# First stages merged into the block of the first head product, and the last layer norm merged into the last feed-forward

## The chip, the cores and the metric

The kernel runs on 1 core of one Trainium2 chip. A core has five engines with a queue of instructions each: TensorE (PE: matrix products and transposes; its weight loads are listed as PEld), VectorE (DVE), ScalarE (ACT), GpSimd (POOL) and SyncE (SP), which here only issues DMA transfers. Engines wait for each other on counting semaphores. The metric is the device time of one execution in microseconds (us); lower is better. The time shown is the median of 3 runs.

## The reference

Two blocks of two layers each run over 512 latent tokens and 256 context tokens of width 1024, in float32. Cut to what the change touches:

```python
# first block, layer 0: the modulation comes out of c, then x is normed and modulated
mod_l = split((silu(c) @ w_mod[i] + b_mod[i])[:, None, :], 6)      # shift, scale, gate, ...
h_l = modulate(rms_norm(x, norm1_g[i]), mod_l[0], mod_l[1])        # h * (1 + scale) + shift
q, k, v = h_l @ w_qkv ...                                          # the first head product
lam = exp(sum(lq1 * lk1)) - exp(sum(lq2 * lk2)) + lam_init

# second block, end of its last layer: feed-forward, residual, layer norm, result
y = layer_norm(ALPHA * x + gate * (square(relu(h @ w1)) @ w2), ln_ff_g, ln_ff_b)

def layer_norm(x, g, b):
    mu = mean(x); var = mean(square(x - mu))
    return (x - mu) * rsqrt(var + LN_EPS) * g + b
```

`rms_norm` is per row of x: it needs x alone, not the modulation. The modulation of layer 0 that the first product needs (shift and scale) is the first 2048 columns of `w_mod`.

## The kernel before

Tokens lie on the 128 partitions: x is six tiles of 128 x 1024 (four latent, two context). Every weight matrix streams through as halves of 128 x 4 x 512 (1024 KB): SP loads a half into `raw[h]`, ACT writes its rounded part `w_hi[h]` (`split_hi`), DVE the rest `w_lo[h]` (`split_lo`), and PE makes each product from three (hi x hi, lo x hi, hi x lo). `raw[h]` is loaded again once the semaphore `lo_done` says that `split_lo` has read it.

The program is a row of blocks. Between two blocks all engines meet at a barrier. Inside `together(K)` several stages share one block, and each engine walks from one stage into the next without a barrier. The order of work is the order of the code on each engine; no planner is involved.

The start has four blocks before:

- The memsets (L887 to L896).
- `start_stage`. SP issues small vectors, the four blocks `mod_first0` to `mod_first3` of `w_mod` (128 x 8 x 512, 2048 KB each), then x (2048 KB) and the context (1024 KB), then both halves of slab 0 and of slab 1 of the first weight stream, and last a bias table that goes to DRAM (`rel_table_rest`), for whose landing it waits. PE multiplies c with each block (`mod_rows`, L852), ACT copies the row out (`first_rows`), PE turns it into columns (`mod_turns`, L860), DVE sums and adds the bias (`mod_sums` L866, `mod_add` L873). ACT and DVE split both halves of slab 0.
- `lambda_stage`: four small DVE operations and one on ACT.
- The `together` block with `scale_stage`, `operand_stage` and `heads_gemm_stage`. `Norm.roots` on ACT takes square, sum and root of each tile of x (L312, L314), `Norm.rest` on DVE the reciprocal (L275) and the scaled tile `xhat` (L282). PE transposes `xhat` (L239), ACT applies scale and shift (`feat`, L804), DVE splits that into `hT_hi` (L761) and `hT_lo` (L763), one of eight groups of 128 features (k = 0 to 7) at a time. PE turns k = 0 to 3 ahead and the others between the products of the first slab's first half (L362 to L364).

`K.held` names a slab whose second half is not split yet when an operand stage begins. `operand_stage` then splits it behind k = 5 on ACT and on DVE. In other places of the program this is in use; at the start it isn't before.

The end has two blocks. In the last chunk of `mlp_stage`, PE makes two halves of the down product for four tiles; DVE multiplies each result with the gate (`scaled_buf`, L535) and POOL adds it to x (L543). Then comes a block of its own, `layer_norm_stage`: statistics of the four tiles on DVE (L1864, L1866), one root on ACT (L1885), and two passes over each tile on DVE (L1869, L1875), behind each of which SP stores the tile.

`Norm.beside` is a way to take a norm inside a product stage, in use elsewhere in the program: behind the gate multiply of tile j (last chunk, second half) DVE takes the statistics of tile j - 1 and writes the normed tile j - 2.

Of the kernel before, what the change touches and what calls it, by code (L numbers as in the profile page):

```python
# [242 lines left out]
class Norm:  # L243


    def __init__(self, K, kind, tiles, out):
        self.kind, self.tiles, self.out = kind, tiles, out
        self.n = len(tiles)
        self.added = None
        self.seen = self.scaled = 0  # L250
# [18 lines left out]
    def normalise(self, K, dve):  # L269
# [29 lines left out]
    def roots(self, K, act):  # L299

        act.preload_act_table(ACT.Sqrt)
        link = Chain(act, K.act_chain)
        for j, t in enumerate(self.tiles):
# [8 lines left out]
            link(act.activation(K.relu_mlp[:, :, :].rearrange("p a b -> p (a b)"), K.x[:, t, :], ACT.Square,  # L312
# [62 lines left out]
def ahead_loop(eng, stage, body, hold=False):  # L375
# [10 lines left out]
    if stage.last:  # L386
# [159 lines left out]
def mlp_stage(K, stream, nxt, tiles, mod=None, hold=False, norm=None):  # L546
# [183 lines left out]
    K.held = st.g0 + 2 * chunks if hold else None  # L730
# [146 lines left out]
def start_stage(K, x, ctx, first, w_mod, groups, rpb, lambdas):  # L877
# [3 lines left out]
    blocks = 4  # L881
    rows = w_mod.rearrange("(k p) n -> p k n", p=P)
    ld0 = [s.n for s in K.mod_loaded]
    us0, tr0, cn0, sm0, ro0, mt0, dc0 = (s.n for s in (K.mod_used, K.turned, K.c_done, K.small_loaded, K.row_out, K.mod_turned,
                                                       K.dve_chain))
    n_vectors = sum(len(g) for g in groups)
# [11 lines left out]
    with nc.Block() as block:  # L898
        @block.sync
        def _(sp):  # L900
            sp.dma_start(K.ident[:, :], K.c_ident).then_inc(K.ident_loaded.h, 16)
# [21 lines left out]
        def _(act):  # L923

            act.wait_ge(K.c_done.h, cn0 + 1)
            act.activation(K.cexp[:, :], K.vecs[:, 0:4 * KD], ACT.Exp, scale=-1.0).then_inc(K.c_done.h, 1)
            for b in range(blocks):
                act.wait_ge(K.mod_used.h, us0 + b + 1)
                act.activation(K.first_rows[:, b, :], K.bank[b][:, :], ACT.Copy).then_inc(K.row_out.h, 1)
            for h in range(2):  # L930
                act.wait_ge(K.raw_loaded[h].h, 16)
                act.activation(K.w_hi[h][:, :, :], K.raw[h][:, :, :], ACT.Copy).then_inc(K.hi_done.h, 1)
            act.wait_ge(K.inputs_loaded.h, 32)

        @block.vector
        def _(dve):
# [17 lines left out]
            ins.then_inc(K.c_done.h, 1)  # L954
            for b in range(blocks):
# [3 lines left out]
            for h in range(2):  # L959
                split_lo(K, dve, 0, h)  # L960
# [3 lines left out]
        def _(pe):  # L964
# [7 lines left out]
            for b in range(blocks):  # L972
                pe.wait_ge(K.mod_loaded[b].h, ld0[b] + 16)
                mod_rows(K, pe, K.bank[b], 0, K.mod_first[b][:, :, :]).then_inc(K.mod_used.h, 1)
# [9 lines left out]
    K.c_done.n += 3  # L984
    K.small_loaded.n += 16 * n_vectors
# [517 lines left out]
def attention_stage(K, units, q_of, k_of, values, out, diff=False, bias=False, sink=False, mod=None):  # L1503
# [35 lines left out]
    with nc.Block() as block:  # L1539
# [6 lines left out]
        elif mod:  # L1546
            @block.sync
            def _(sp):
                for v, p in rows_at.items():
                    if p >= 1:  # L1550
                        sp.wait_ge(K.pt_done[0].h, at(K.pt_done[0], order[v - len(units) // PAIRS, "mod"]))
                    sp.dma_start(K.mod_slab[:, :, :], mod.w[:, :, (mod.first + 4 * p) * P:(mod.first + 4 * p + 4) * P])\
                      .then_inc(K.mod_loaded[0].h, 16)
                    skew_bias(K, sp, (2 * p, 2 * p + 1))
# [285 lines left out]
def layer_norm_stage(K, gain, bias, tiles, store=None, gate=None, gate_scale=1.0):  # L1840


    nc = K.nc
    n = len(tiles)
    classes = 2 if n > LAT_TILES else 1
    mm0 = K.mm_done.n
    sm0, st0, sd0, rs0, ga0 = K.small_loaded.n, K.sums_done.n, K.std_done.n, K.rstd_done.n, K.gained.n
    with nc.Block() as block:
        @block.sync
        def _(sp):  # L1850
            sp.dma_start(K.ln_gain[:, :], gain.partition_broadcast(P)).then_inc(K.small_loaded.h, 16)
            sp.dma_start(K.ln_bias[:, :], bias.partition_broadcast(P)).then_inc(K.small_loaded.h, 16)
            if store is not None:
                for i, t in enumerate(tiles):
                    sp.wait_ge(K.gained.h, ga0 + i + 1)
                    sp.dma_start(store[t * P:(t + 1) * P, :], K.x[:, t, :]).then_inc(K.stored.h, 16)
                sp.wait_ge(K.stored.h, K.stored.n + 16 * n)

        @block.vector
        def _(dve):  # L1860
            link = Chain(dve, K.dve_chain)
            for i, t in enumerate(tiles):
                for h in range(2):
                    ins = dve.bn_stats(K.ln_stats[:, t, h, :], K.x[:, t, h * 512:(h + 1) * 512])  # L1864
                    link(ins)
                dve.bn_aggr(K.ln_mv[:, t, :], K.ln_stats[:, t, :, :]).then_inc(K.sums_done.h, 1)  # L1866
            dve.wait_ge(K.small_loaded.h, sm0 + 32)
            for i, t in enumerate(tiles):
                link(dve.scalar_tensor_tensor(K.x[:, t, :], K.x[:, t, :], K.ln_mv[:, t, 0:1], K.ln_gain[:, :],  # L1869
                                              ALU.subtract, ALU.mult))  # L1870
                if i == 0:
                    dve.wait_ge(K.std_done.h, sd0 + 1)
                    dve.reciprocal(K.rstd[:, 0:n], K.lnms[:, 0:n]).then_inc(K.rstd_done.h, 1)  # L1873
                    dve.wait_ge(K.rstd_done.h, rs0 + 1)
                dve.scalar_tensor_tensor(K.x[:, t, :], K.x[:, t, :], K.rstd[:, t:t + 1], K.ln_bias[:, :], ALU.mult, ALU.add)\  # L1875
                   .then_inc(K.gained.h, 1)
            K.dve_chain.n += link.k

        @block.scalar
        def _(act):  # L1880
            act.preload_act_table(ACT.Sqrt)
            if gate is not None:
                gate_evacuations(K, act, mm0, classes, gate_scale)
            act.wait_ge(K.sums_done.h, st0 + n)
            act.activation(K.lnms[:, 0:n], K.ln_mv[:, 0:n, 1], ACT.Sqrt, bias=K.eps_ln[:, 0:1]).then_inc(K.std_done.h, 1)  # L1885
        if gate is not None:
            @block.tensor
            def _(pe):
                for cls in range(classes):
                    gate_rows(K, pe, gate, cls)  # L1890
    if gate is not None:
        K.mm_done.n += classes
        K.gate_done.n += 2 * classes
    K.small_loaded.n += 32
    for s in (K.sums_done, K.gained):
        s.n += n
    K.std_done.n += 1
    K.rstd_done.n += 1
    if store is not None:
# [1346 lines left out]
```

## Time and profile before

| | us |
|---|---|
| median of 3 runs | 4089.12 |
| lowest and highest | 4088.18, 4091.37 |
| the profiled execution | 4090.46 |
| its span | 4088.7 |
| PE busy | 3773.7 (92%) |
| DVE busy | 1986.6 (49%) |
| ACT busy | 1330.2 (33%) |
| POOL busy | 807.5 (20%) |

The span is what the trace covers, from the first instruction to the last event; the profiled execution's own time is 1.76 us longer. PE is busy in nearly all of the span, so the places where it isn't are the ones to look at: in the page's picture of 40 slices (102 us each) the first slice of PE is 3 tenths. The last one is 7.

### The profile page before, as it was taken

The numbers are of one execution on the slowest core, as the hardware profiler recorded it, in microseconds if no ns is written. First come the engines' busy times: TensorE is split into PE (matmuls) and PEld (weight loads), VectorE is DVE, ScalarE is ACT, GpSimd is POOL, SyncE is SP. The second block draws the span as 40 slices with busy tenths as digits, with TensorE's granted clock in tenths as the row PEclk, the third lists the DMA queues.
The fourth block names the chain that finished last, engine by engine and source line by source line (L and its number), as shares of the span: only waits on it lengthen the run. The fifth ranks groups of instructions, "written<-read, shape, count | busy, mean of one in ns | idle before, by whom it ended". The sixth has DMA issues, their size and how long they took to land. (4 is left out here: it accounts for less than half of the span.)

```text
span 4088.7 us, 54795 instructions
## 1 busy us (share of the span) xinstructions
PE 3773.7 (92%) x20683; PEld 3018.8 (74%) x20683; DVE 1986.6 (49%) x2911; ACT 1330.2 (33%) x2276; POOL 807.5 (20%) x604
## 2 busy tenths in 40 slices
PE   3998889999999899999999999999999988898997
PEld 2875578888877667777776678888878865577776
DVE  2746644333354375443436654333356727746444
ACT  2335533212143354322325522122224324432222
POOL 0510011221222111122220011212110018701222
PEclk8999989999999899999999999999999998999999
DMA  4125303322312220444320013323211140032222
GB/s 159 55 72 150 98 31 115 122 92 97 118 52 72 83 53 32 175 144 154 103 75 3 2 42 128 123 92 123 92 62 52 55 144 14 19 103 83 92 92 72
DMA packets 191734, 352.34 MB, mean 86 GB/s; under 512 B 41980, under 2 KB 43597, under 8 KB 191565
## 3 DMA queue, kind: packets, MB, share of 16 engines
q1 hardware_dynamic: 189277, 346.07, 25.7%
q10 hardware_dynamic: 2304, 4.20, 0.3%
q8 instruction: 100, 1.64, 0.2%
q14 instruction: 53, 0.43, 0.0%
HBM read 341.71 MB, written 16.92 MB: 88 GB/s over the span
## 5 line engine op out<-in xcount | busy, mean ns | idle before, releaser
L543 POOL TENSOR_TENSOR x<-x,scaled_buf 128x512 f32<-128x512 f32 (+1 forms) x360 | 466.8, 1301 | 2335.4 <-DVE scaled_buf L535 2334.8
L129 DVE TENSOR_TENSOR w_lo<-raw,w_hi 128x2048 fp32r<-128x2048 f32 x198 | 457.8, 2312 | 827.9 <-ACT w_hi L123 809.7
L123 ACT ACTIVATE w_hi<-raw 128x2048 fp32r<-128x2048 f32 x196 | 375.3, 1915 | 1223.6 <-PE psum L364 1221.2
L362 PE MATMUL psum<-hT_hi,w_hi 128*128 128x256 f32 (+1 forms) x1920 | 677.6, 353 | 3.3 <-DVE hT_lo L763 2.5
L363 PE MATMUL psum<-hT_lo,w_hi 128*128 128x256 f32 (+1 forms) x1920 | 673.9, 351 | 0.0
L364 PE MATMUL psum<-hT_hi,w_lo 128*128 128x256 f32 (+1 forms) x1920 | 673.8, 351 | 0.0
L362 PE MATMUL psum<-w_hi,uT_hi 128*128 128x512 f32 x1280 | 512.4, 400 | 17.1 <-DVE uT_lo L614 17.1
L535 DVE TENSOR_TENSOR scaled_buf<-psum,gate 128x512 f32<-128x512 f32 x360 | 246.9, 690 | 538.5 <-PE psum L364 533.7
L364 PE MATMUL psum<-w_hi,uT_lo 128*128 128x512 f32 x1280 | 506.3, 396 | 0.0
L363 PE MATMUL psum<-w_lo,uT_hi 128*128 128x512 f32 x1280 | 506.3, 396 | 0.0
L362 PE MATMUL psum<-w_hi,hT_hi 128*128 128x512 f32 x1072 | 420.0, 392 | 8.3 <-ACT qkv L1250 5.9
L364 PE MATMUL psum<-w_hi,hT_lo 128*128 128x512 f32 x1072 | 417.5, 390 | 0.0
L363 PE MATMUL psum<-w_lo,hT_hi 128*128 128x512 f32 x1072 | 417.4, 389 | 0.0
L362 PEld LDWEIGHTS psum<-hT_hi,w_hi 128*128 128x128 f32 x1920 | 364.2, 190 | 52.6 <-DVE hT_lo L763 2.9
L363 PEld LDWEIGHTS psum<-hT_lo,w_hi 128*128 128x128 f32 x1920 | 364.1, 190 | 48.4
L364 PEld LDWEIGHTS psum<-hT_hi,w_lo 128*128 128x128 f32 x1920 | 363.5, 189 | 48.7
L362 PEld LDWEIGHTS psum<-w_hi,uT_hi 128*128 128x128 f32 x1280 | 240.7, 188 | 88.8 <-DVE uT_lo L614 24.0
L364 PEld LDWEIGHTS psum<-w_hi,uT_lo 128*128 128x128 f32 x1280 | 240.7, 188 | 57.9
L363 PEld LDWEIGHTS psum<-w_lo,uT_hi 128*128 128x128 f32 x1280 | 240.8, 188 | 54.2
L362 PEld LDWEIGHTS psum<-w_hi,hT_hi 128*128 128x128 f32 x1072 | 201.5, 188 | 51.7 <-ACT qkv L1250 7.5
L364 PEld LDWEIGHTS psum<-w_hi,hT_lo 128*128 128x128 f32 x1072 | 201.3, 188 | 41.9
L363 PEld LDWEIGHTS psum<-w_lo,hT_hi 128*128 128x128 f32 x1072 | 201.4, 188 | 40.8
(279 smaller groups left out, 4775.7 us busy)
## 6 DMA issues: line engine op xcount, KB each, us to landing
mod_wide<-in_w_mod SPq DMA_DIRECT2D x24, 3072.0 KB, 10.6
raw<-in_w_mlp SPq DMA_DIRECT2D x64, 1024.0 KB, 5.3
raw<-in_ff_w SPq DMA_DIRECT2D x64, 1024.0 KB, 5.3
raw<-in_ssm_w_in SPq DMA_DIRECT2D x20, 1024.0 KB, 5.1
mod_slab<-in_w_mod SPq DMA_DIRECT2D x8, 2048.0 KB, 8.1
raw<-in_a_w_qkv SPq DMA_DIRECT2D x12, 1024.0 KB, 5.1
raw<-in_b_w_qkv SPq DMA_DIRECT2D x12, 1024.0 KB, 5.1
mod_first<-in_w_mod SPq DMA_DIRECT2D x4, 2048.0 KB, 17.9
```

Source lines behind the costliest of these rows:

```text
L123: act.activation(K.w_hi[h][:, :, :], K.raw[h][:, :, :], ACT.Copy).then_inc(K.hi_done.h, 1)
L129: dve.tensor_tensor(K.w_lo[h][:, :, :], K.raw[h][:, :, :], K.w_hi[h][:, :, :].bitcast(F32), ALU.subtract).then_inc(K.lo_done.h, 1)
L362: pe.matmul(out, hi_a, hi_w, start=first, stop=False, **check)
L363: pe.matmul(out, hi_a, lo_w, start=False, stop=False, **check)
L364: return pe.matmul(out, lo_a, hi_w, start=False, stop=last, **check)
L535: dve.tensor_tensor(K.scaled_buf[:, j % 2, :], bank[:, :], K.gate[:, cls, ds(n * SLAB_N, SLAB_N)], ALU.mult)\
L543: pool.tensor_tensor(x, x, K.scaled_buf[:, j % 2, :], ALU.add).then_inc(K.added.h, 1)
```

## The change

- The memsets stay in a block of their own (`clear_stage`). `start_stage` moves into the `together` block, the lambda operations move into it, and the barriers between fall away. PE waits at its end for DVE's chain of sums.
- SP's order: x and the context come ahead of the modulation blocks; there are three buffers for the four modulation blocks, so the fourth is loaded into the first buffer once PE has read it. The bias table goes out in the midst of them. Slab 0's second half is loaded once all roots are taken (their squares go to that buffer), slab 1 behind it.
- The roots of x come ahead of the `first_rows` copies on ACT; the scaled tiles come on DVE behind the third block's product and ahead of the sums. They are written to `xhat_far`, which doesn't overlap the three buffers.
- Slab 0's second half is split as a held half (`K.held = 0`).
- The last layer norm becomes a `Norm` of kind "layer" with gain and bias rows, taken beside the last chunk's gate multiplies and finished in `store_stage`, in the same block. The two rows are loaded earlier, behind the last operand.

```diff
 class Norm:
     def normalise(self, K, dve):
...
-        if self.kind == "layer":
+        if self.rows is not None:
+            gain, bias = self.rows
+            link = Chain(dve, K.dve_chain)
+            if j == 0:
+                dve.wait_ge(K.small_loaded.h, self.loaded)
+            link(dve.scalar_tensor_tensor(self.out[:, t, :], K.x[:, t, :], K.ln_mv[:, t, 0:1], gain[:, :], ALU.subtract, ALU.mult))
+            ins = dve.scalar_tensor_tensor(self.out[:, t, :], self.out[:, t, :], K.rstd[:, t:t + 1], bias[:, :], ALU.mult, ALU.add)
+            K.dve_chain.n += link.k
+        elif self.kind == "layer":
...
 def start_stage(...)
-            for b in range(blocks):
-                sp.dma_start(K.mod_first[b][:, :, :], rows[:, :, b * SLAB_N:(b + 1) * SLAB_N]).then_inc(K.mod_loaded[b].h, 16)
             sp.dma_start(K.x[:, 0:LAT_TILES, :], x.rearrange("(t p) n -> p t n", p=P)).then_inc(K.inputs_loaded.h, 16)
             sp.dma_start(K.x[:, LAT_TILES:TOK_TILES, :], ctx.rearrange("(t p) n -> p t n", p=P)).then_inc(K.inputs_loaded.h, 16)
-            for n in range(2):
-                for h in range(2):
-                    load_half(K, sp, n, h, first.half(n, h), first=n == 0)
+            mod_block(0)
             sp.wait_ge(K.dve_chain.h, dc0 + 1)
             sp.dma_start(K.rel_dram.rearrange("(h r c) -> h r c", r=REL_ROWS + 2, c=P), K.rel_table[:, :, :]).then_inc(K.rel_loaded.h, 16)
-            sp.wait_ge(K.rel_loaded.h, 32)
+            mod_block(1)
+            mod_block(2)
+            load_half(K, sp, 0, 0, first.half(0, 0), first=True)
+            sp.wait_ge(K.mod_used.h, us0 + 1)
+            mod_block(3)
+            sp.wait_ge(K.std_done.h, norm.sd0 + norm.n)
+            load_half(K, sp, 0, 1, first.half(0, 1), first=True)
+            for h in range(2):
+                load_half(K, sp, 1, h, first.half(1, h))
...
         def _(act):
+            act.wait_ge(K.dve_chain.h, dc0 + 5)
+            act.activation(K.lam_sum[:, :], K.lam_sum[:, :], ACT.Exp).then_inc(K.act_chain.h, 1)
+            act.wait_ge(K.inputs_loaded.h, 32)
+            norm.roots(K, act)
             for b in range(blocks):
                 act.wait_ge(K.mod_used.h, us0 + b + 1)
                 act.activation(K.first_rows[:, b, :], K.bank[b][:, :], ACT.Copy).then_inc(K.row_out.h, 1)
-            for h in range(2):
-                act.wait_ge(K.raw_loaded[h].h, 16)
-                act.activation(K.w_hi[h][:, :, :], K.raw[h][:, :, :], ACT.Copy).then_inc(K.hi_done.h, 1)
-            act.wait_ge(K.inputs_loaded.h, 32)
+                if b == 2:
+                    act.wait_ge(K.raw_loaded[0].h, 16)
+                    act.activation(K.w_hi[0][:, :, :], K.raw[0][:, :, :], ACT.Copy).then_inc(K.hi_done.h, 1)
...
         def _(dve):
+            dve.wait_ge(K.inputs_loaded.h, 32)
+            dve.wait_ge(K.mod_used.h, us0 + 3)
+            norm.rest(K, dve)
+            split_lo(K, dve, 0, 0)
             for b in range(blocks):
                 dve.wait_ge(K.mod_turned.h, mt0 + b + 1)
                 link(mod_sums(K, dve, K.bank[b], 4))
                 link(mod_add(K, dve, 0, 4 * b, 4))
-            for h in range(2):
-                split_lo(K, dve, 0, h)
+            dve.wait_ge(K.rel_loaded.h, 32)
...
+            pe.wait_ge(K.dve_chain.h, K.dve_chain.n)
+    K.held = 0
...
-            mlp(latent)
-        layer_norm_stage(K, A["ln_ff_g_2"][1], A["ln_ff_b_2"][1], latent, store=out)
+            row_loads(K, ((K.out_gain[:, :], A["ln_ff_g_2"][1]), (K.out_bias[:, :], A["ln_ff_b_2"][1])), (K.feat_lo.h, K.feat_lo.n))
+            norm = Norm(K, "layer", latent, K.x, rows=(K.out_gain, K.out_bias))
+            mlp(latent, norm=norm)
+            store_stage(K, norm, out)
```

SP's queue at the start, before, from the bias table's load on (`mod_first0` to `3` are the modulation blocks, `raw0` and `raw1` the two weight halves):

```order
L910 DMA rel_table_131<-in_b_rpb 16x15x31
L912 DMA mod_first0_85<-in_w_mod 128x8x512
L912 DMA mod_first1_86<-in_w_mod 128x8x512
L912 DMA mod_first2_87<-in_w_mod 128x8x512
L912 DMA mod_first3_88<-in_w_mod 128x8x512
L913 DMA x_49<-in_x 128x4x1024
L914 DMA x_49<-in_ctx 128x2x1024
L116 DMA raw0_52<-in_a_w_qkv 128x4x512
L116 DMA raw1_53<-in_a_w_qkv 128x4x512
L116 DMA raw0_52<-in_a_w_qkv 128x4x512
L116 DMA raw1_53<-in_a_w_qkv 128x4x512
L919 DMA rel_table_rest<-rel_table_131 16x2176
```

And in the changed kernel:

```order
L935 DMA rel_table_130<-in_b_rpb 16x15x31
L936 DMA x_49<-in_x 128x4x1024
L937 DMA x_49<-in_ctx 128x2x1024
L924 DMA mod_first0_85<-in_w_mod 128x8x512
L940 DMA rel_table_rest<-rel_table_130 16x2176
L924 DMA mod_first1_86<-in_w_mod 128x8x512
L924 DMA mod_first2_87<-in_w_mod 128x8x512
L116 DMA raw0_52<-in_a_w_qkv 128x4x512
L924 DMA mod_first0_85<-in_w_mod 128x8x512
L116 DMA raw1_53<-in_a_w_qkv 128x4x512
L116 DMA raw0_52<-in_a_w_qkv 128x4x512
L116 DMA raw1_53<-in_a_w_qkv 128x4x512
```

x and the context moved from behind the last modulation block to ahead of the first; slab 0's first half moved ahead of the last modulation block.

DVE's queue at the end, before, from the last `split_lo` of the program on:

```order
L129 TENSOR_TENSOR w_lo_57<-raw_53,w_hi_55 128x2048
L535 TENSOR_TENSOR scaled_buf<-psum,gate 128x512 x8
L175 UNCONDITIONAL_BRANCH
L1859 UNCONDITIONAL_BRANCH
L1864 BN_STATS ln_stats<-x 128x6 x2
L1866 BN_AGGR ln_mv<-ln_stats 128x2
```

And in the changed kernel, from the same place on:

```order
L551 TENSOR_TENSOR scaled_buf<-psum,gate 128x512 x6
L268 BN_STATS ln_stats<-x 128x6 x2
L270 BN_AGGR ln_mv<-ln_stats 128x2
L551 TENSOR_TENSOR scaled_buf<-psum,gate 128x512
L268 BN_STATS ln_stats<-x 128x6 x2
L270 BN_AGGR ln_mv<-ln_stats 128x2
L278 RECIPROCAL rstd<-lnms 128x1
L287 SCALAR_TENSOR_TENSOR x<-x,ln_mv,out_gain 128x1024
L288 SCALAR_TENSOR_TENSOR x<-x,rstd,out_bias 128x1024
L551 TENSOR_TENSOR scaled_buf<-psum,gate 128x512
L268 BN_STATS ln_stats<-x 128x6 x2
L270 BN_AGGR ln_mv<-ln_stats 128x2
```

The statistics of the first three tiles and the two passes over the first moved in between the last three gate multiplies; behind these rows come the passes over tile 1, and then tile 3's statistics and the passes over tiles 2 and 3.

## Rows read from the trace of the kernel before

**Rows 1.** Windows, core 0: length, busy us (instructions) by engine, granted clock, DMA share, GB/s.

```profile
0.00:86.00 86.00, 20.35 (x108) 8.89 (x108) 19.84 (x41) 20.77 (x34) 2.21 (x9) 0.80 0.52 189
86.00:4067.00 3981.00, 3753.30 (x20578) 3009.94 (x20576) 1950.26 (x2850) 1307.88 (x2241) 804.07 (x594) 0.98 0.26 84
```

**Rows 2.** Timeline of SP's queue at the start: start us, us, engine, line, what [idle before].

```profile
30.69 5.29 SPq L913 DMA_DIRECT2D x<-in_x  x1
...
62.96 0.50 SPq L919 DMA_DIRECT2D rel_table_rest<-rel_table  x1
```

**Rows 3.** Timeline of all engines, modulation and first splits.

```profile
29.17 3.59 PE L852 MATMUL psum<-mod_first,cT 128*2 128x512 f32 x16 [11.95 <-DMA mod_first<-in_w_mod]
...
39.93 1.90 PE L852 MATMUL psum<-mod_first,cT 128*2 128x512 f32 x16 [1.84 <-DMA mod_first<-in_w_mod]
...
45.33 3.50 PE L852 MATMUL psum<-mod_first,cT 128*2 128x512 f32 x16 [3.50 <-DMA mod_first<-in_w_mod]
...
51.06 0.17 DVE L873 TENSOR_TENSOR modT_all<-mod_sum,vecs 128x8 f32<-128x8 f32 x1
55.71 1.91 ACT L932 ACTIVATE w_hi<-raw 128x2048 fp32r<-128x2048 f32 x1 [6.21 <-DMA raw<-in_a_w_qkv]
57.72 2.29 DVE L129 TENSOR_TENSOR w_lo<-raw,w_hi 128x2048 fp32r<-128x2048 f32 x1 [6.50 <-ACT w_hi L932]
```

**Rows 4.** Timeline of all engines, from the first norm into the first product.

```profile
71.46 1.06 ACT L312 ACTIVATE relu_mlp<-x 128x1024 f32<-128x1024 f32 x1
...
79.80 0.17 DVE L275 RECIPROCAL rstd<-lnms 128x1 f32<-128x1 f32 x1 [0.41 <-ACT lnms L314]
80.00 0.75 DVE L282 TENSOR_SCALAR xhat<-x,rstd 128x1024 f32<-128x1024 f32 x1
...
80.90 5.35 PE L239 MATMUL psum<-ident,xhat 128*128 128x128 f32 x24 [30.17 <-DVE xhat L282]
...
85.90 0.59 PE L362 MATMUL psum<-w_hi,hT_hi 128*128 128x512 f32 x1
...
88.18 0.82 PE L239 MATMUL psum<-ident,xhat 128*128 128x128 f32 x6
...
97.57 0.56 DVE L761 CAST hT_hi<-feat 128x768 fp32r<-128x768 f32 x1 [3.20 <-ACT feat L804]
```

**Rows 5.** Windows around the changes of the granted clock (columns as in Rows 1).

```profile
48.00:49.00 1.00, 1.00 (x10) 0.24 (x3) 0.00 (x0) 0.10 (x1) 0.00 (x0) 0.70 1.03 410
...
55.00:56.00 1.00, 0.00 (x0) 0.00 (x0) 0.00 (x0) 0.29 (x1) 0.00 (x0) 0.71 1.04 381
...
81.00:86.00 5.00, 5.00 (x25) 5.00 (x25) 2.58 (x4) 3.44 (x6) 0.00 (x0) 0.50 0.02 3
86.00:87.00 1.00, 1.00 (x6) 0.85 (x5) 0.97 (x3) 0.77 (x2) 0.00 (x0) 0.93 0.00 0
```

**Rows 6.** Timeline at the end of the program, DVE and POOL.

```profile
4063.99 0.69 DVE L535 TENSOR_TENSOR scaled_buf<-psum,gate 128x512 f32<-128x512 f32 x1 [2.11 <-PE psum L364]
...
4066.78 0.69 DVE L535 TENSOR_TENSOR scaled_buf<-psum,gate 128x512 f32<-128x512 f32 x1 [2.11 <-PE psum L364]
4067.55 1.26 POOL L543 TENSOR_TENSOR x<-x,scaled_buf 128x512 f32<-128x512 f32 x1 [1.50 <-DVE scaled_buf L535]
...
4079.33 1.28 DVE L1875 SCALAR_TENSOR_TENSOR x<-x,rstd,ln_bias 128x1024 f32<-128x1024 f32 x1
...
4084.36 1.28 DVE L1875 SCALAR_TENSOR_TENSOR x<-x,rstd,ln_bias 128x1024 f32<-128x1024 f32 x1
```

**Rows 7.** Timeline of DVE in other feed-forwards that have a norm beside them.

```profile
1180.89 1.81 DVE L282 TENSOR_SCALAR xhat_far<-x,rstd 128x1024 f32<-128x1024 f32 x1
...
3005.47 0.68 DVE L535 TENSOR_TENSOR scaled_buf<-psum,gate 128x512 f32<-128x512 f32 x1
...
3007.64 0.11 DVE L275 RECIPROCAL rstd<-lnms 128x1 f32<-128x1 f32 x1
3007.78 0.81 DVE L280 TENSOR_SCALAR x<-x,ln_mv,rstd 128x1024 f32<-128x1024 f32 x1
```

More of the change, by code:

```diff
@@ L243, with __init__ @@
 class Norm:
-    def __init__(self, K, kind, tiles, out):
+    def __init__(self, K, kind, tiles, out, rows=None, junk=None):
         self.kind, self.tiles, self.out = kind, tiles, out
+        self.rows, self.loaded = rows, K.small_loaded.n
         self.n = len(tiles)
         self.added = None
+        self.rooted = False
+        self.junk = junk or K.relu_mlp[:, :, :]
         self.seen = self.scaled = 0
@@ L299, in roots @@
     def roots(self, K, act):
+        if self.rooted:
+            return
+        self.rooted = True
         act.preload_act_table(ACT.Sqrt)
@@ L385, in ahead_loop @@
             body(i, True)
-    if stage.last:
+    if stage.last and hold:
+        body(n - 1, False, True)
+    elif stage.last:
         body(n - 1, False)
@@ L729, in _ @@
                 chunk(c, False)
-    K.held = st.g0 + 2 * chunks if hold else None
+    K.held = st.g0 + 2 * chunks if hold and not st.last else None
     K.mm_done.n += 3 * (nt - 1) * chunks
@@ L874, in mod_add, with clear_stage @@
                              K.vecs[:, ds(n0 + b_at, count)].unsqueeze(2).to_broadcast([P, count, 2]), ALU.add)
-def start_stage(K, x, ctx, first, w_mod, groups, rpb, lambdas):
+def clear_stage(K):
     nc = K.nc
[L881 to L886, printed above, removed]
     with nc.Block() as block:
@@ L896, in _, with start_stage, mod_block @@
             pool.memset(K.rel_table[:, :, :], 0.0)
-    with nc.Block() as block:
+def start_stage(K, x, ctx, first, w_mod, groups, rpb, lambdas, norm):
+    nc = K.nc
+    blocks = 4
+    rows = w_mod.rearrange("(k p) n -> p k n", p=P)
+    ld0 = [s.n for s in K.mod_loaded]
+    us0, tr0, cn0, sm0, ro0, mt0, dc0 = (s.n for s in (K.mod_used, K.turned, K.c_done, K.small_loaded, K.row_out, K.mod_turned,
+                                                       K.dve_chain))
+    n_vectors = sum(len(g) for g in groups)
+    ac0 = K.act_chain.n
+    with engines(K) as block:
         @block.sync
         def _(sp):
+            def mod_block(b):
+                sp.dma_start(K.mod_first[b % 3][:, :, :], rows[:, :, b * SLAB_N:(b + 1) * SLAB_N]).then_inc(K.mod_loaded[b].h, 16)
             sp.dma_start(K.ident[:, :], K.c_ident).then_inc(K.ident_loaded.h, 16)
@@ L973, in _ @@
                 pe.wait_ge(K.mod_loaded[b].h, ld0[b] + 16)
[L974 removed]
+                mod_rows(K, pe, K.bank[b], 0, K.mod_first[b % 3][:, :, :]).then_inc(K.mod_used.h, 1)
             for b in range(blocks):
@@ L1837, in split_stage, with store_stage, _ @@
     K.feed = Feed(fl0, (K.gate_done.h, K.gate_done.n))
[L1840 to L1848, printed above, removed]
+def store_stage(K, norm, out):
+    with engines(K) as block:
+        @block.scalar
+        def _(act):
+            norm.roots(K, act)
+        @block.vector
+        def _(dve):
+            norm.rest(K, dve)
@@ L1849, in _ @@
         @block.sync
         def _(sp):
[L1851 to L1899, printed above, removed]
-        K.stored.n += 16 * n
+            for j, t in enumerate(norm.tiles):
+                sp.wait_ge(K.normed.h, norm.nr0 + j + 1)
+                sp.dma_start(out[t * P:(t + 1) * P, :], norm.out[:, t, :]).then_inc(K.stored.h, 16)
+            sp.wait_ge(K.stored.h, K.stored.n + 16 * norm.n)
@@ L1904 @@
+    K.stored.n += 16 * norm.n
 TAPS = 5
@@ L2766, in program @@
         c = Cursor(R)
-        K.mod_first = [c.put(f"mod_first{b}", [P, KD, SLAB_N]) for b in range(4)]
+        K.mod_first = [c.put(f"mod_first{b}", [P, KD, SLAB_N]) for b in range(3)]
+        c = Cursor(qkv_end)
         K.vec_in = c.put("vec_in", [P, 3, P])
@@ L3052, in program @@
         flat = lambda name: A[name].rearrange("l n -> (l n)")
[L3053 to L3057 removed]
+        norm = Norm(K, "square", every, K.xhat_far, junk=K.raw[1][:, 0:2, :])
+        clear_stage(K)
         of_layer(0)
         with together(K):
+            start_stage(K, A["x"][0], A["ctx"][0], streams[0], A["w_mod"][0],
+                        ((A["c"][0], A["c_ctx"], A["c_2"][0], A["c_ctx_2"], flat("norm1_g"), flat("norm2_g"), A["a_subln_g"][0],
+                          flat("ln_mix_g_2"), flat("ln_mix_b_2"), A["ln_ff_g_2"][0], A["ln_ff_b_2"][0]),
+                         (flat("b_mod"),), (flat("b_mod_2"),)), A["b_rpb"][0], [A[f"a_lambda_{n}"][0] for n in ("q1", "k1", "q2", "k2")],
+                        norm)
             scale_stage(K, 1, NORM1_AT)
[L3061 removed]
+            operand_stage(K, far_at, KD, True, K.hT_hi, K.hT_lo, **modulated(0), norm=norm)
             heads_gemm_stage(K, **next_streams(), parts=((0, 2, every, 0), (2, 4, every, 1), (4, 6, every, None)),
```

42 lines of the change are left out of this document (12 added, 30 removed).

## The prediction, made before the changed kernel had run

> **What bounds the kernel now.** I read the windows first, then the timelines of the two ends. From 86 to 4067 us TensorE is busy for 3753.3 of 3981.0 us [rows 1]; the change touches nothing there but a split half and two small loads, and every weight load in that stretch is released by the splits and so moves along with the products. Before 86 us TensorE is busy for 20.35 us [rows 1]: a shift of the first product to an earlier time shortens the whole program by as much. The reader is to see the same at the end: the last gate multiply starts at 4066.78 and DVE's last pass ends at 4084.36 + 1.28 = 4085.64 [rows 6], with TensorE done. So two waits matter: what the first product at 85.90 [rows 4] waits for, and what the last store waits for.
>
> At the start, the transfers set the pace until 55.71, when ACT begins on the first weight half [rows 3]. The modulation was complete at 51.06 + 0.17 = 51.23 [rows 3] and TensorE had nothing from there to 80.90 [rows 4]. In between lie two splits, an issue of the bias table at 62.96 [rows 2], its landing, a barrier, the lambda operations, and a norm that begins at 71.46 and ends at 80.75 [rows 4]. x itself had come long before: only the order of the code keeps its norm behind all this.
>
> **The start, part by part.** *Transfers.* Up to the fourth modulation block the changed queue holds 2048 KB of x, 1024 KB of context, three blocks of 2048 KB, 1024 KB of weights and a fourth block of 2048 KB: 12288 KB. In the kernel before, the first weight half is the end of just as many (4 x 2048 + 2048 + 1024 + 1024), and it was there at 55.71 [rows 3]. The bias table, 136 KB, now goes out in the midst: at 0.41 MB a microsecond [rows 5] 0.35 us. The fourth block is there at 56.1. The third block is the end of 9 x 1024 KB; the fourth was the end of 8 at 45.33 and 12 were there at 55.71, so 2.6 us for each: 45.3 + 2.6 + 0.35 = 48.3.
>
> The fourth block waits for its buffer: the first block is the end of 5 x 1024 KB, thus some 37 us, and 3.59 us of rows follow it: 41 us. By then 5 x 1024 KB lie ahead of it in the queue, until about 51, so the wait is hidden with 10 us to spare; even an issue as long as that of x, 5.29 us [rows 2], would end at 46. If that cover were gone each microsecond would count in full.
>
> *ACT.* The roots of x took 71.46 to about 79.8 [rows 4], 8.3 us and a table load ahead of them; now they lie between the context's landing (the end of 3 x 1024 KB, some 32) and 42, while blocks 1 and 2 arrive. ACT is then about 1 us late for block 0's copy, which nobody waits for: TensorE turns only after the fourth block. The split of the first half (1.91) lies at about 52 to 54.
>
> *DVE.* Behind the third block's rows (48.3 + 3.59 = 51.9) come six tiles. Each costs 0.20 from reciprocal to scaling and 0.75 for it [rows 4], 0.95, in all 5.7: 57.6. The split of the first half adds 2.29 [rows 3]: 59.9. The lambda operations come well ahead of the third block, where DVE has nothing else to do: nothing.
>
> *The last wait.* TensorE ends the fourth block's rows at 56.1 + 3.50 = 59.6 if its clock is low as at 45.33, or at 58.0 if it is high as at 39.93 (1.90) [rows 3]; DVE is free for the sums at 59.9. The two are nearly even. From the end of the rows to the last sum it took 51.23 - (45.33 + 3.50) = 2.40 us: 62.0. Transposes can start at 62.1.
>
> *From transposes to the first product.* Before: 80.90 to 85.90, 5.0 us, with the 24 transposes taking 5.35 at a granted clock of 0.50 [rows 4, 5]. At the full clock six take 0.82 [rows 4], 24 take 3.3. The clock's level is the choice here. Before, the rows from 45.33 on raised it within 48 to 49 us, and it fell only in 55 to 56 [rows 5], 6 us or more after the rows had ended. The new transposes begin 2.5 us behind the rows, so I take the full clock: 3.3 us for them, or 3.8 with ACT's and DVE's first feature behind the first four. The first product comes at 65.9, against 85.90: **20.0 us less**; at the low clock it would be 67.1 and 18.8.
>
> *The held half.* Its split (ACT 1.91, DVE 2.29) now lies behind feature 5, where before DVE was idle for 3.20 us ahead of feature 6 [rows 4], and TensorE needs it only after the 72 products of the first half. Slab 1's second half is loaded behind that and is needed when both halves of slab 0 are through. I count nothing; if the cover were gone, DVE's 2.29 would count.
>
> **The end.** Before, nothing of the norm begins until the barrier behind the last add. Now DVE, from the third tile's gate multiply at 4063.99 on, is never idle. Gate multiply and statistics take 3007.64 - 3005.47 = 2.17 us, reciprocal to the next pass 0.14 [rows 7], two passes over a tile (4084.36 - 4079.33) / 2 = 2.52 [rows 6]. So: tile 2's multiply, statistics of tile 1 and passes of tile 0: 4063.99 + 2.17 + 0.14 + 2.52 = 4068.8. That delays the last multiply by 2.0 us behind its 4066.78. The same again for it: 4073.7. Tile 3's statistics without a multiply, 2.17 - 0.68 = 1.5: 4075.1. Two tiles of 2.66: 4080.5, with the last pass's end at 4080.6 against 4085.64: **5.0 us less**. The stores behind it are as before. The roots, 0.3 us each, lie beside passes or statistics; POOL's last add ends 2.0 us after its multiply begins [rows 6], before the third tile's statistics do (2.17), so its result isn't waited for.
>
> The page "SBUF — State Buffer" of the Trainium skill (section "SBUF: two separate sides") speaks against this: a DVE operation with two SBUF inputs and a GpSimd operation lock each other out for a whole instruction. Row 1180.89 agrees: a scaling took 1.81 us beside an add, against 0.75 alone [rows 4, 7]. By the working above each add ends while DVE takes statistics, 0.3 us before the next pass with two inputs; if they met, 1.0 us would be lost, once or twice.
>
> **Sum.** 4088.7 - 20.0 - 5.0 = 4063.7 for the span. The profiled execution took 4090.46, 1.76 more than its span, and 1.3 more than the median; the median moves to 4089.12 - 25.0 = **4064.1**.
>
> **Rivals.**
> *The clock is low* in the transposes, or falls at their end and has to rise again. For it: a fall in 55 to 56 [rows 5] when the rows had ended at 48.8, by which it might fall at 66, just as products begin. Against: TensorE's pause between rows and transposes is short. Price: 1.2 us for the transposes, and at most five microseconds of products at half speed (81 to 86 was as long [rows 5]), 2.3: 4065.3 to 4067.6. The skill's page "TensorE: Matmul & The Clock Gate" (section "Part 4: PE-mode transpose") says that transposes don't count as work for the clock. The trace agrees so far: 0.50 through 5 us of them, 0.93 in the microsecond of the first product. By it the clock could only fall in the new start; chance below.
>
> *DVE ends last at the start*: each scaling takes 1.81 us as beside adds [rows 7], 1.06 more, six times that 6.4. Against it: POOL is idle there. 4070.5; for half of it, 4067.
>
> *The fourth block comes late* since SP is held up or the stream leaves a gap: 3 to 5 us, 4067 to 4069.
>
> *Little of it arrives.* The program's later stages wait for something that doesn't move with the products, so half of the start's gain is given back: 4074. If almost all of it is (under 8 us left), no change can be told. For this nothing in the trace speaks: TensorE is busy 94% from 86 to 4067.
>
> *Slower.* TensorE's clock doesn't rise when the first head product starts, since there is no longer a dense run of transposes right ahead at a settled level. At the low level rows take 3.50 for 1.90 [rows 3], 0.84 us more for each of full-speed work; the 25 us are eaten once 30 us of full-speed work run at the low level, and with 40 us the kernel is 8.6 us slower, 4098. Against it: the clock was at 0.93 within the microsecond of the first product.
>
> **How the numbers follow.** Forecast 62%; low clock 12%; DVE last 9%; fourth block late 6%; half given back 5%; nothing to be told 4%; slower 2%. Within 0.2% (8 us, about what a measurement of this kernel can tell from no change) lies only the sixth. Faster by more: 94%. The range is from 4060.5 (high clock in the rows, DVE's 0.75 hidden, executions 1 us apart) to 4069.5, which takes in the first three rivals but for the worst of the second.
>
> **What would show it.** Right: x and context landed at about 32; the fourth `mod_rows` starts at 56; the last `modT_all` sum ends at 62; first product of L376 at 66; no idle PE before the slab's second half; the last L288 ends 20 us plus 5 earlier than 4085.6, with the last gate multiply 2 us later than TensorE's result. Wrong: a product start later than 68, PE idle time between 66 and 130 for `w_lo` or `raw`, passes of more than 1.3 us at the end, or a granted clock of 0.50 after 67.

## The result, and the profile after

The changed kernel takes 4067.77 us (median of 5 runs, 4061.82 to 4069.37) against 4088.18 for the kernel before on the same chip (5 runs, 4087.06 to 4091.37): a ratio of 0.9944, 95% interval 0.9934 to 0.9955, so 18 to 27 us less. Forecast were 4064.1, 25.0 less, and a range of 4060.5 to 4069.5. The profiled execution of the changed kernel took 4063.22, its span is 4061.4; the span before was 4088.7. Of two kernels in the experiments one execution each (9552 and 5024 us) was a slow one, and all medians and ratios leave it out.

The span falls into three stretches: up to the first head product; from there to the gate multiply of the third tile in the last chunk ("middle"); from there to the end ("end"). All times are starts in us.

| | first product | middle | third gate multiply | end | span |
|---|---|---|---|---|---|
| before | 85.90 | 3978.09 | 4063.99 | 24.7 | 4088.7 |
| after | 65.74 | 3974.98 | 4040.72 | 20.7 | 4061.4 |
| difference | 20.2 | 3.1 | | 4.0 | 27.3 |

The start, timeline of all engines (columns as in [rows 3]; repeated rows left out). These answer to [rows 3] and [rows 4]:

```profile
30.53 1.28 ACT L315 ACT_TABLE_LOAD   x1 [3.68 <-DMA x<-in_ctx]
...
36.02 3.33 PE L868 MATMUL psum<-mod_first,cT 128*2 128x512 f32 x16 [18.76 <-DMA mod_first<-in_w_mod]
...
40.03 0.58 ACT L963 ACTIVATE first_rows<-psum 128x512 f32<-128x512 f32 x1
...
47.12 3.59 PE L868 MATMUL psum<-mod_first,cT 128*2 128x512 f32 x16 [2.47 <-DMA mod_first<-in_w_mod]
...
50.84 0.16 DVE L278 RECIPROCAL rstd<-lnms 128x1 f32<-128x1 f32 x1 [23.48 <-PE psum L868]
51.03 0.75 DVE L293 TENSOR_SCALAR xhat_far<-x,rstd 128x1024 f32<-128x1024 f32 x1
...
55.25 3.59 PE L868 MATMUL psum<-mod_first,cT 128*2 128x512 f32 x16 [4.54 <-DMA mod_first<-in_w_mod]
...
56.00 2.29 DVE L129 TENSOR_TENSOR w_lo<-raw,w_hi 128x2048 fp32r<-128x2048 f32 x1
58.77 2.27 PE L876 MATMUL psum<-ident,first_rows 128*128 128x128 f32 x16
...
59.77 0.19 DVE L882 TENSOR_REDUCE mod_sum<-psum 128x8 f32<-128x32 f32 x1 [1.48 <-PE psum L876]
...
61.38 0.17 DVE L889 TENSOR_TENSOR modT_all<-mod_sum,vecs 128x8 f32<-128x8 f32 x1
...
61.93 2.81 PE L239 MATMUL psum<-ident,xhat_far 128*128 128x128 f32 x24 [0.89 <-DVE modT_all L889]
...
65.74 0.47 PE L376 MATMUL psum<-w_hi,hT_hi 128*128 128x512 f32 x1 [1.00 <-DVE hT_lo L779]
...
77.34 0.56 DVE L777 CAST hT_hi<-feat 128x768 fp32r<-128x768 f32 x1 [0.65 <-ACT feat L820]
```

TensorE's 30.17 us of idle time ahead of the transposes [rows 4] has become 0.89. The whole norm on DVE (50.84 to 56.0) now lies beside the wait for the last modulation weights. The windows (columns as in [rows 1]) say the same, and that TensorE runs without a gap at the full clock once products begin:

```profile
43.00:59.00 16.00, 8.99 (x41) 1.04 (x34) 7.24 (x13) 3.09 (x4) 0.00 (x0) 0.50 0.91 333
...
61.00:66.00 5.00, 3.11 (x26) 2.89 (x26) 2.82 (x9) 2.78 (x5) 0.00 (x0) 1.00 0.37 143
...
66.00:86.00 20.00, 20.00 (x101) 16.58 (x101) 12.14 (x14) 10.94 (x15) 0.00 (x0) 1.00 0.18 56
```

The end, timeline of DVE and POOL, which answers to [rows 6]:

```profile
4040.72 0.69 DVE L551 TENSOR_TENSOR scaled_buf<-psum,gate 128x512 f32<-128x512 f32 x1 [0.54 <-PE psum L378]
...
4043.04 1.28 DVE L287 SCALAR_TENSOR_TENSOR x<-x,ln_mv,out_gain 128x1024 f32<-128x1024 f32 x1
...
4045.56 0.68 DVE L551 TENSOR_TENSOR scaled_buf<-psum,gate 128x512 f32<-128x512 f32 x1
...
4046.33 1.26 POOL L559 TENSOR_TENSOR x<-x,scaled_buf 128x512 f32<-128x512 f32 x1 [3.53 <-DVE scaled_buf L551]
...
4047.88 1.28 DVE L287 SCALAR_TENSOR_TENSOR x<-x,ln_mv,out_gain 128x1024 f32<-128x1024 f32 x1
...
4056.16 1.28 DVE L288 SCALAR_TENSOR_TENSOR x<-x,rstd,out_bias 128x1024 f32<-128x1024 f32 x1
```

DVE's last pass ends 16.72 us after the third tile's multiply begins; before it was 21.65. That is 4.9 less, but the stretch to the end is only 4.0 shorter. The rest is in the last store. In the transfers of the last 4.2 us, before has no row for instructions and its landing takes 2.6 us:

```profile
q1 hardware_dynamic: 234, 0.83, 48.8%
issues: line engine op xcount, KB each, median us to landing
out<-x SPq DMA_DIRECT2D x1, 512.0 KB, 2.6
```

After, a fetch of instructions stands beside it, and it takes 3.6:

```profile
q1 hardware_dynamic: 144, 0.52, 31.7%
q14 instruction: 1, 0.01, 0.5%
issues: line engine op xcount, KB each, median us to landing
out<-x SPq DMA_DIRECT2D x1, 512.0 KB, 3.6
```

### The profile page after: what moved, and what is told of

Same layout as the page of the kernel before. It is cut to its first block and busy times, and to the rows that moved or that the text cites. A ratio compares the mean times of both kernels' runs of the same rounds, so it can differ in the third digit from the quotient of the medians.

```text
span 4061.4 us, 54770 instructions
## 1 busy us (share of the span) xinstructions
PE 3768.1 (93%) x20683; PEld 3010.1 (74%) x20683; DVE 1985.6 (49%) x2914; ACT 1332.0 (33%) x2279; POOL 807.4 (20%) x604
```

## The experiments

"First product", "middle", "end" and "landing" (of the last store) are as above. Ratios are to the kernel before on the same chip, with their 95% intervals.

| | first product | middle | end | landing | median | ratio |
|---|---|---|---|---|---|---|
| changed kernel, again | 65.43 | 3977.91 | 20.7 | 3.6 | 4065.85 | 0.9943 (0.9931 to 0.9956) |
| start alone | 65.61 | 3977.74 | 24.7 | 2.6 | 4069.97 | 0.9953 (0.9941 to 0.9966) |
| end alone | 85.19 | 3977.91 | 19.8 | 2.6 | 4082.05 | 0.9985 (0.9976 to 0.9994) |
| norm behind the modulation | 75.34 | 3975.1 | 19.8 | 2.6 | 4073.58 | 0.9954 (0.9939 to 0.9969) |
| x loaded last | 69.86 | 3979.5 | 19.8 | 2.6 | 4068.86 | 0.9943 (0.9928 to 0.9958) |
| first half late | 64.31 | 3977.14 | 20.7 | 3.6 | 4065.77 | 0.9946 (0.9933 to 0.9958) |
| 24 memsets | 67.30 | 3976.6 | 19.8 | 2.6 | 4064.82 | 0.9935 (0.9920 to 0.9950) |
| split behind the scale | 63.21 | 3975.2 | 20.7 | 3.6 | 4062.30 | 0.9930 (0.9916 to 0.9943) |
| the same, again | 61.43 | 3975.28 | 20.7 | 3.6 | 4058.72 | 0.9926 (0.9913 to 0.9940) |
| and 24 memsets | 64.45 | 3974.85 | 19.8 | 2.6 | 4060.21 | 0.9928 (0.9908 to 0.9948) |
| and 8 memsets | 62.74 | 3970.34 | 19.8 | 2.6 | 4055.13 | 0.9921 (0.9905 to 0.9938) |
| the same, again | 64.26 | 3978.71 | 19.8 | 2.6 | 4058.64 | 0.9924 (0.9911 to 0.9938) |

**The two parts, each alone, and the whole again.** The kernel of "start alone" keeps the old last stage:

```diff
-            mlp(latent, norm=norm)
-            store_stage(K, norm, out)
+            mlp(latent)
+        layer_norm_stage(K, A["ln_ff_g_2"][1], A["ln_ff_b_2"][1], latent, store=out)
```

"End alone" keeps the old start: x behind four blocks in four buffers, and both halves of slab 0 split ahead. Against the changed kernel:

```diff
-        clear_stage(K)
+        start_stage(...)
+        lambda_stage(K)
...
-            operand_stage(K, far_at, KD, True, K.hT_hi, K.hT_lo, **modulated(0), norm=norm)
+            operand_stage(K, xhat_at, KD, True, K.hT_hi, K.hT_lo, **modulated(0), norm=Norm(K, "square", every, K.xhat))
```

> The changed kernel once more, nothing edited. Of the 27.3 us by which the profiled span shrank, 20.2 lie ahead of the first product and 4.0 behind the last gate multiply but one; 3.1 us lie in between, where nothing was changed. Theory A: those 3.1 us are one low stretch of the granted clock less (3.4 us each), and the last store landed 1.0 us late because one 8 KB instruction fetch shared a DMA engine with it; both are chance. Then this profile has its first product within 1 us of 65.7 and another number of low stretches, its middle differs from 3975.0 us by 0 to 4 us, and the times spread over some 7 us as before. Theory B: the 3.1 us belong to the change; then the middle is 3975 within 0.5 us again.

> The start's part of the change alone: the old last feed-forward and the separate last layer norm are kept. Theory (the two parts add): first product at 65.7 as in the changed kernel, the stretch from the multiply at 4063.99 to the end 24.7 us as in the kernel before; time 20 us below before (4068), 4 to 5 above the changed kernel. Rival (a shift of the start is partly given back in the middle): less than 17 us below before.

> The end's part alone: the old start is kept, the last layer norm is taken beside the last gate multiplies. Theory: first product at 85.9; from the third tile's gate multiply to DVE's last pass 16.7 us, to the end of the span 19.7 (20.7 if an instruction fetch meets the last store again); time 5 us below before if the store lands in 2.6 us, 4 if in 3.6. Rival (the slower landing belongs to the merged end, since the code of the end is fetched later): 20.7 again, 4 us.

The parts don't touch each other: the start alone gives 85.90 - 65.61 = 20.3 us, and its end is 24.7 as before; the end alone gives 24.7 - 19.8 = 4.9 with the first product at 85.19. The end alone gains the full 4.9 on DVE, the whole only 4.0: the landing of the whole is 3.6 in both profiles, so this is no accident of one execution, as theory A had it. The 3.1 us of the middle are an accident: they were gone in the second profile of the same kernel. The clock goes with them. By the records of the granted clock in the three traces TensorE was at its low level for 177.7 us of the middle before, for 170.7 in the first profile of the changed kernel and for 177.5 in the second.

**What hides the norm, and what the order of transfers is worth.** In "norm behind the modulation" the roots on ACT and the scaled tiles on DVE follow the last block; in "x loaded last" x and context follow all four blocks too, with slab 0's first half and its split behind them:

```diff
-            act.wait_ge(K.inputs_loaded.h, 32)
-            norm.roots(K, act)
             for b in range(blocks):
                 ...
+            act.wait_ge(K.inputs_loaded.h, 32)
+            norm.roots(K, act)
```

```diff
-            sp.dma_start(K.x[:, 0:LAT_TILES, :], ...)
-            sp.dma_start(K.x[:, LAT_TILES:TOK_TILES, :], ...)
             ...
-            load_half(K, sp, 0, 0, first.half(0, 0), first=True)
             ...
             mod_block(3)
+            sp.dma_start(K.x[:, 0:LAT_TILES, :], ...)
+            sp.dma_start(K.x[:, LAT_TILES:TOK_TILES, :], ...)
+            load_half(K, sp, 0, 0, first.half(0, 0), first=True)
```

> The merged start with the norm put back behind the modulation: on ACT the roots come behind the first_rows copies, on DVE the split comes first, then the sums, then the scalings. Transfers as in the changed kernel. Theory (the norm is hidden only because of its place in the order): roots start when the last first_rows copy ends, 59.5, with 1.3 of table load and 8.2 of roots, last scaling ends at 70.2, transposes at 70.3 at the low clock, first product at 75.3: 9.6 us later than 65.7, still 10.6 earlier than 85.9. Rival (the barriers and the lambda block were most of the start's loss, the norm would be hidden anyway): first product before 70.

> The merged start with x and the context loaded behind the four modulation blocks and slab 0's first half behind them; the roots on ACT and the scalings on DVE come behind the modulation, then the splits. Theory (loading x first is worth little by itself; it is worth what its norm and the split then take behind the last transfer): context lands at 53.3, roots until 62.8, split until 67.0, first product at 70.4, 4.7 us later than 65.7. Rival (the stream of 12288 KB is the bound in both, so the order of loads does not matter): first product at 66 to 67.

The first came out at 75.34. Timeline of it, from the sixth scaled tile on:

```profile
69.44 0.75 DVE L293 TENSOR_SCALAR xhat_far<-x,rstd 128x1024 f32<-128x1024 f32 x1
70.34 5.36 PE L239 MATMUL psum<-ident,xhat_far 128*128 128x128 f32 x24 [9.52 <-DVE mod_scale L1055]
...
75.34 0.72 PE L376 MATMUL psum<-w_hi,hT_hi 128*128 128x512 f32 x1
```

So of the 20.2 us, 9.6 are the norm's place in the order on ACT and DVE (75.34 - 65.74), and the other 10.6 the rest of the start: the barriers, the lambda block, the wait for the bias table, one split instead of two, and the new order of the transfers, which no run takes apart. The transposes begin after 9.52 us without work and take 5.36 at a granted clock of 0.50, as before [rows 4, 5], where after a pause of 0.89 they took 2.81 at 1.00. From their start to the first product it is 5.00 instead of 3.81, so 1.2 of the 9.6 are the clock's. The second came out at 69.86, 4.1 us later than the changed kernel but 5.5 earlier than the first. Both have the norm behind the modulation, so x and the weight half ahead of the blocks by themselves lose: without 4 x 1024 KB ahead of it the last block comes some 4 x 2.6 = 10.4 us sooner, and TensorE was through with its turns at 50.14 there, at 61.04 in the changed kernel. Only together with the norm's new place, which needs x early, does the order pay, and both together are worth the 4.1 us.

**The split of the first half.** In the changed kernel it stands before the sums, and its load before the fourth block. "First half late" puts both behind, and lets DVE scale the tiles as soon as their roots are there; "split behind the scale" moves the split on DVE once more, behind `scale_stage`. The first of them:

```diff
-            load_half(K, sp, 0, 0, first.half(0, 0), first=True)
             sp.wait_ge(K.mod_used.h, us0 + 1)
             mod_block(3)
+            load_half(K, sp, 0, 0, first.half(0, 0), first=True)
...
-            split_lo(K, dve, 0, 0)
             for b in range(blocks):
                 ...
+            split_lo(K, dve, 0, 0)
```

> The changed kernel with three moves at the start: slab 0's first half is loaded behind the fourth modulation block and not ahead of it, DVE scales the tiles as soon as their roots are there, and the split of the half comes behind the sums. Theory (the fourth block's landing sets the first product): its rows start 2.6 us earlier, at 52.6, sums end at 59, transposes start at 59; the split now ends at about 61, so the first product comes at 62.6, 3.1 us earlier than 65.7. Rival (DVE's row of work sets it: scalings and split ended at 58.3, 1.5 us before the first sum): the split behind the sums takes all of it back, first product at 65 or later.

> v_half_late with one more move: DVE takes the two operations of scale_stage ahead of slab 0's split and not behind it. In v_half_late the first feature waited for them until 61.23 while the transposes ran from 58.97. Theory: first feature at 59.3, done at 60.7; the split ends at 61.3, then cast and rest until 62.9; first product at 62.9, 1.4 earlier than v_half_late's 64.31 and 2.8 earlier than the changed kernel's; the time 2.8 us below the changed kernel's, which the spread of 6 us may hide. Rival (DVE is the bound whatever the order): 64.3 again.

The first gave 64.31 and not 62.6. Its timeline names what was overlooked:

```profile
52.65 3.03 PE L868 MATMUL psum<-mod_first,cT 128*2 128x512 f32 x16 [2.25 <-DMA mod_first<-in_w_mod]
...
58.61 2.29 DVE L129 TENSOR_TENSOR w_lo<-raw,w_hi 128x2048 fp32r<-128x2048 f32 x1
58.97 2.81 PE L239 MATMUL psum<-ident,xhat_far 128*128 128x128 f32 x24 [0.89 <-DVE modT_all L889]
...
61.23 2.36 ACT L820 ACTIVATE feat<-psum,modT_all,mod_scale 128x512 f32<-128x512 f32 x4 [3.10 <-DVE mod_scale L1062]
```

The fourth block comes 2.6 us sooner (52.65 against 55.25) and the transposes too, but ACT's first feature needs `mod_scale`, which DVE now makes behind the split: the wait has moved from PE to ACT. With the split one step later the feature is released by the transposes:

```profile
59.04 2.81 PE L239 MATMUL psum<-ident,xhat_far 128*128 128x128 f32 x24 [0.89 <-DVE modT_all L889]
59.21 2.28 DVE L129 TENSOR_TENSOR w_lo<-raw,w_hi 128x2048 fp32r<-128x2048 f32 x1
59.77 2.35 ACT L820 ACTIVATE feat<-psum,modT_all,mod_scale 128x512 f32<-128x512 f32 x4 [1.79 <-PE psum L239]
...
63.21 0.46 PE L376 MATMUL psum<-w_hi,hT_hi 128*128 128x512 f32 x1 [1.36 <-DVE hT_lo L779]
```

63.21, 2.5 less than the changed kernel. Not all of it is the order's: the rows of the fourth block took 2.81 us here and 3.59 there, as the clock stood. The same kernel once more had them at 1.90 and its first product at 61.43. With memsets (below) it had them at 3.24, 3.59 and 3.59 and came at 62.74, 64.26 and 64.45; the last is 1.25 from 63.2, just outside what was expected. Free of this is the stretch from the start of the transposes: 4.17 us to the first product with the split behind the scale, 5.34 with the split ahead of it.

**The fetch beside the last store.** The memsets stand on DVE in its wait of 23.48 us and only move its later code:

```diff
+            for i in range(24):
+                link(dve.memset(K.mod_sum[:, 0:1, :], 0.0))
             dve.wait_ge(K.inputs_loaded.h, 32)
```

> The changed kernel with 24 small memsets on DVE put ahead of the scalings, where DVE is idle for 23 us. They cost nothing there; they only shift DVE's later code by 24 instructions. In the changed kernel, the same again and v_half_late the last store landed in 3.6 us with one instruction fetch of 8 KB beside it, in e_end and e_start in 2.6 without one. Theory (it is DVE's code whose fetch falls on the last store): the fetch comes earlier, the last store lands in 2.6 us and the stretch from the multiply of the third tile to the end of the span is 19.7 instead of 20.7. Rival (another engine's code): 20.7 and 3.6 as before.

> The version with the split behind the scale, and 24 small memsets in DVE's idle time before the scaled tiles (about 3 us there, in a wait of over 20 us), which move all of DVE's later code. Theory (the last store lands late because a fetch of DVE's code falls beside it): the landing is 2.6 us instead of 3.6, the stretch from the third tile's gate multiply to the end 19.8 instead of 20.7, first product within 1 us of 63.2. Rival (the late landing belongs to the merged end itself, and the earlier padded kernel missed it by chance): 3.6 and 20.7 as in the version without memsets.

> The same with 8 memsets. It tells how far the code has to move: if the fetch goes already with 8, landing 2.6 and last stretch 19.8; if a shift by 8 instructions is too little to move a fetch past the end of the program, 3.6 and 20.7. Both are open under the theory; under the rival it is 3.6 here and with 24 alike. First product within 1 us of 63.2 in any case.

With 24 memsets in either kernel, and with 8, the landing is 2.6 and the end 19.8; without them it was 3.6 and 20.7 in all five profiles of the three kernels with the whole change and DVE's norm ahead of the sums; the two that move the norm behind them have 2.6 too. The transfers at the end of the changed kernel with 24 memsets hold no fetch:

```profile
q1 hardware_dynamic: 212, 0.74, 43.6%
issues: line engine op xcount, KB each, median us to landing
out<-x SPq DMA_DIRECT2D x1, 512.0 KB, 2.6
```

The 1.0 us thus depends on where DVE's code lies, and not on the merged end, which "end alone" has too. By the traces the last fetch of this queue starts 1.8 us ahead of the end of the span in the five with 3.6; 8 memsets move it to 14.5 or 14.7 us ahead of the end and 24 to 19.1 or 19.4. In the two with the norm behind the sums it comes 1.1 us behind the end, though DVE does the same work; why is not shown, and neither is how a fetch of 0.3 us costs the store 1.0.

The first product of the changed kernel with 24 memsets came 1.6 us later than in the changed kernel, which was not expected: 0.8 us of that were there from the bias table's landing on, ahead of the memsets, and 0.7 came with turns that took 2.92 us instead of 2.27.

**The middle.** The kernel with the split behind the scale and 8 memsets had a middle 4.5 us shorter than any before it, and 4054.64 to 4057.96 in four runs. So it and its unpadded twin ran once more:

> The version with the split behind the scale and 8 memsets, again. In its first profile the middle (first product to the third tile's gate multiply) took 3970.3 us, where all kernels before it had 3975 to 3979.5; 4.7 us of that lie between 240 and 350 us, where its trace has one low-clock stretch of 3 us and the others 17 to 20 us of them in sum. Theory A (where TensorE's clock falls there is chance, run by run): the middle is 3975 to 3979 this time and the median 4058 to 4061. Theory B (the program's timing settles it, and 8 memsets happen to give a good one): the middle is 3970 to 3972 again and the median 4054 to 4057. In both the last store's landing is 2.6 and the last stretch 19.8.

> The version without memsets again, on the same chip. Theory A: its median is within 2 us of that of the padded one, but for 1.0 us of the last landing (3.6 against 2.6). Theory B: 4060 to 4063, 5 to 7 us above the padded one, middle 3975 or more.

Theory A held: the same kernel now had a middle of 3978.71, 8.4 us more, and the two medians are 4058.64 and 4058.72. One window shows where the first difference lies. First profile:

```profile
240.00:350.00 110.00, 91.65 (x583) 69.33 (x583) 58.33 (x100) 51.35 (x111) 0.00 (x0) 0.97 0.37 112
```

Second profile of the same kernel:

```profile
240.00:350.00 110.00, 91.81 (x540) 68.65 (x538) 54.50 (x93) 47.65 (x102) 0.00 (x0) 0.91 0.39 115
```

TensorE is busy as long in both, but does 583 instructions in the one and 540 in the other: at a granted clock of 0.97 and 0.91. The low level was granted for 6.8 us of this window in the first (in two stretches; the expectation above speaks of one) and for 20.5 in the second; over the middle for 160.4 and 180.9. The changed kernel has 0.91 there too. How long the clock is low in the middle differs from execution to execution of one kernel.

## Why the prediction was right

By its own steps:

- *Transfers and the fourth block.* Forecast 48.3 and 56.1 for the third and fourth, measured 47.12 and 55.25: each about 1 us early. The wait for the first buffer was hidden, as argued. Right.
- *ACT.* Context at 30.53 (some 32), block 0's copy at 40.03, 0.7 us after its rows ended at 39.35 (about 1). Right.
- *DVE.* Free at 56.00 + 2.29 = 58.29 instead of 59.9: 1.2 from the earlier end of the third block's rows (50.71 for 51.9), the rest from tiles at 0.86 us each instead of 0.95. The scalings took 0.75; the rival that had them at 1.81 is out.
- *The last wait.* Rows ended at 58.84 (59.6), and DVE then waited 1.48 us for the first turns: TensorE's side was last, DVE not. The last sum ended at 61.55 (62.0), 2.71 behind the rows where the working had 2.40, since the turns took 2.27 us. The choice "nearly even" went to TensorE.
- *Transposes.* Begun at 61.93 (62.1), at the full clock, 2.81 us (3.3), and 3.81 us to the first product (3.8). The choice of the full clock was the right one. Its argument had one row too few: before, TensorE was at its turns from 48.76 to 50.73, so the clock fell some 5 us behind its last work, not 6 or more behind the rows. The pause that counted here was 0.89 us, and that is short by either count. The rows of the fourth block ran at the low clock (3.59), the price of that was in the sum.
- *First product.* 65.74 against 65.9, 20.2 less against 20.0. That it is this close is in part luck: the fourth block came 0.85 us early, and longer turns and a later start behind the sums took most of that back.
- *Held half.* DVE's idle time ahead of feature 6 fell from 3.20 [rows 4] to 0.65 us, and TensorE is busy for 20.00 of 20.00 us from 66 to 86 and for 64.00 of 64.00 from 66 to 130. Nothing, as counted; 0.65 us of cover are left.
- *The end on DVE.* Last pass 16.72 us behind the third tile's multiply, forecast 16.6. The last multiply at 4045.56 is 2.1 late (2.0). The last add ends at 4047.59, 0.29 before the next pass with two inputs; no pass took more than 1.28. The lockout that was feared didn't come, and it wasn't tried either: no pass met an add. Row 1180.89, which the prediction gave for it, is of an operation that reads one tensor of SBUF, not two.
- *"The stores behind it are as before."* This was wrong by 1.0 us: the fetch.
- *The sum.* 25.0 forecast. The profile shows 27.3, of which 24.2 belong to the change (20.2 + 4.0) and 3.1 to the clock in the middle. The two comparisons of medians show 20.4 and 23.1, intervals from 18 to 28. Runs of the changed kernel lie up to 7.6 us apart, those of the kernel before up to 12, so a forecast of 25.0 can't be told from 24.2 by times; the places in the trace can tell it.

The rivals: a low clock in the transposes was seen only in kernels in which TensorE had paused longer ahead of them (5.36 and 5.10 us, with the norm late), and its price was the 1.2 us of the forecast. A late fourth block, gain given back and a slower kernel were not seen: "start alone" has its first product 20.3 us and its third gate multiply 20.6 us earlier than before.

The lowest times are those of the split behind the scale: 4062.30 and 4058.72 in two comparisons, 0.9930 and 0.9926, with memsets 0.9921 to 0.9928. Their intervals overlap with those of the changed kernel (0.9944 and 0.9943), so that it is faster rests on the profiles: against 65.74 its first product is 1.3 to 4.3 us earlier in five of them, memsets or not, and the least with the fourth block's rows at 3.59 us in both. What the memsets add (1.0 us by the profile) is too small for these times.

## What to carry to other kernels

A norm that needs only the input belongs into the wait for the weights. Loading the input first is not enough: with the norm still behind the modulation the start was 5.5 us slower than with x and the weight half loaded last; with the norm moved as well it was 4.1 faster. When a large operation is moved behind a short chain, follow each small result of that engine, not only the sums that TensorE waits for: the scale behind the split cost 1.2 us here (5.34 against 4.17 from transposes to first product). Add up the stretches of a trace by marks that belong to the program; what differs between them from one execution to the next of the same kernel isn't the change's.

## What the hardware showed that was not expected

- With a fetch of one packet of instructions beside it the last 512 KB store landed in 3.6 us (five profiles), without one in 2.6 (nine). 8 memsets far ahead of it on DVE were enough to be rid of it.
- The transposes of one and the same stage took 2.81 us after pauses of TensorE of 0.89 to 1.29 us, and 4.45 to 5.36 us after pauses of 9.52 to 31.91.
- The middle of one kernel took 3970.34 us in one execution and 3978.71 in another, with the granted clock of one stretch of 110 us at 0.97 and 0.91.
- The first product of one kernel came at 63.21 us in one execution and at 61.43 in another, with the rows of the fourth modulation block at 2.81 and 1.90 us. A gain of one or two microseconds at the start can be the clock's.
